# Twelve tiles of a product moved forward into the last two groups of a recurrence

## The reference

```
u = rmsnorm(x) @ w_in                       # 1024 -> 3072
xb, gate = u[..., :1536], u[..., 1536:]
xb = causal_depthwise_conv(xb)              # 4 taps along the sequence
r = sigmoid(xb @ wr + br)                   # 16 blocks of 96 x 96
i = sigmoid(xb @ wi + bi)
a = exp(-8 * r * softplus(-lam))
b = sqrt(1 - a * a) * (i * xb)
hs = scan(h[t] = a[t] * h[t-1] + b[t])      # along the sequence
x = x + (hs * silu(gate)) @ w_out           # 1536 -> 1024, the output product
```

## Time and profile before

| what | value |
|---|---|
| median of three runs | 1154.45 us |
| profiled execution | 1155.51 us |
| its span on the core | 1153.7 us |
| TensorE matmul busy | 1130.5 us, 98% |
| VectorE busy | 637.5 us, 55% |
| ScalarE busy | 519.3 us, 45% |
| GpSimd busy | 159.0 us, 14% |
| granted TensorE clock, mean | 0.996 |
| weight loads | 180 of 512 KB, 3.4 us from issue to landing |

### The profile page before, as it was taken

The page is one execution under the profiler, slowest core; times in us unless marked ns, Lnnn a source line. Parts: engine busy times, 40 slices in busy tenths (PEclk is TensorE's granted clock), DMA queues, the critical chain, the costliest instruction groups (busy, mean ns, idle before and its releaser), DMA issues.

```text
span 1153.7 us, 14370 instructions
## 1 busy us (share of the span) xinstructions
PE 1130.5 (98%) x5342; PEld 889.1 (77%) x5342; DVE 637.5 (55%) x1083; ACT 519.3 (45%) x904; POOL 159.0 (14%) x198
## 2 busy tenths in 40 slices
PE   9999889999999999999999999999999999999997
PEld 6787667887666678867777778888888888888886
DVE  7787887854567665455545544555454232544232
ACT  6656656544566544244434433334443211443231
POOL 2022112310223212032202210012000000000021
PEclk9999999999999999999999999999999999999999
DMA  6323222332111123212223123323223223223312
GB/s 225 110 73 91 92 73 92 110 110 74 55 56 55 37 77 107 97 52 71 91 74 111 59 70 101 101 92 107 95 91 109 92 93 106 90 95 103 98 55 74
DMA packets 30806, 102.82 MB, mean 89 GB/s; under 512 B 3344, under 2 KB 5648, under 8 KB 30736
## 3 DMA queue, kind: packets, MB, share of 16 engines
q1 hardware_dynamic: 30304, 101.37, 27.0%
q10 hardware_dynamic: 432, 0.52, 0.1%
HBM read 99.78 MB, written 2.10 MB: 88 GB/s over the span
## 4 chain that ended last, share of the span: by engine, by line
PE 84%; DVE 9%; ACT 5%; issue 2%; DMA 1%; SPq 0%; DVEq 0%; ACTq 0%
PE ps L693 25%; PE ps L695 24%; PE ps L694 24%; PE ps L817 3%; PE ps L829 2%; PE ps L860 2%; DVE xs L1253 2%; DVE wl L1178 1%; DVE Pt L1384 1%; ACT wh L892 1%; ACT Pt L1057 1%; DVE sg L1269 1%; PE ps L854 1%; DVE cc L1285 1%; PE ps L765 1%
## 5 line engine op out<-in xcount | busy, mean ns | idle before, releaser
L693 PE MATMUL ps<-xgh,wh 128*128 128x512 f32 x848 | 348.8, 411 | 7.9 <-DVE wl L1178 6.9
L695 PE MATMUL ps<-xgh,wl 128*128 128x512 f32 x848 | 332.6, 392 | 0.0
L694 PE MATMUL ps<-xgl,wh 128*128 128x512 f32 x848 | 332.0, 392 | 0.0
L1178 DVE TENSOR_TENSOR wl<-raw,wh 128x1024 fp32r<-128x1024 f32 x180 | 229.5, 1277 | 133.7 <-ACT wh L892 131.9
L892 ACT ACTIVATE wh<-raw 128x1024 fp32r<-128x1024 f32 x180 | 188.5, 1049 | 129.6 <-PE ps L695 128.9
L693 PEld LDWEIGHTS ps<-xgh,wh 128*128 128x128 f32 x848 | 160.1, 189 | 59.0 <-issue 29.5
L695 PEld LDWEIGHTS ps<-xgh,wl 128*128 128x128 f32 x848 | 159.8, 188 | 34.4
L694 PEld LDWEIGHTS ps<-xgl,wh 128*128 128x128 f32 x848 | 160.3, 189 | 32.4 <-issue 3.4
L1638 POOL TENSOR_SCALAR Pt<-Pt,stat 128x256 f32<-128x256 f32 (+2 forms) x128 | 74.7, 596 | 296.4 <-DVE stat L1416 217.8
L1057 ACT ACTIVATE Pt<-Pt,stat 128x256 f32<-128x256 f32 (+2 forms) x128 | 64.7, 506 | 107.6 <-DVE stat L1388 42.2
L693 PE MATMUL ps<-fh,wh 128*128 128x512 f32 x240 | 93.5, 389 | 0.0
(11 more groups left out here) (219 smaller groups left out, 1582.1 us busy)
## 6 DMA issues: line engine op xcount, KB each, us to landing
raw<-wst SPq DMA_DIRECT2D x180, 512.0 KB, 3.4
bst<-nbias SPq DMA_DIRECT2D x8, 256.0 KB, 4.1
xt<-xT SPq DMA_DIRECT2D x3, 512.0 KB, 7.7
outT<-ot SPq DMA_DIRECT2D x2, 384.0 KB, 2.5
outT<-ot SPq DMA_DIRECT2D x6, 128.0 KB, 2.0
raw<-wst SPq DMA_DIRECT2D x2, 256.0 KB, 4.0
cstt<-cst SPq DMA_DIRECT2D x1, 512.0 KB, 5.8
xt<-xT ACTq DMA_DIRECT2D x1, 256.0 KB, 3.6
```

Source lines behind the costliest of these rows:

```text
L693: e.matmul(o, high, a, start=(k == 0), stop=False)
L694: e.matmul(o, high, b, start=False, stop=False)
L695: e.matmul(o, low, a, start=False, stop=stop).then_inc(tile_done, 1)
L1178: e.tensor_tensor(wl_t[:, u % NHL, :], raw_t[:, u % NRAW, :], f32(wh_t[:, u % NHL, :]), ALU.subtract).then_inc(lo_done, 1)
```

## The change

Two accumulators of the output product, `wa` 0 and 1, are opened before the recurrence ends and stay open in banks 7 and 6. In group three their tiles k = 0 to 2 are run, in group four k = 3 to 5: those of `wa` 0 before the conv tiles, those of `wa` 1 between the conv and the gate half. Each of the two groups so holds 64 tiles; the third is tiles 116 to 179, the fourth 180 to 243. Behind the last gates `wa` 0 and 1 run k = 6 to 8 and `wa` 2 and 3 k = 0 to 8 (24 tiles, 244 to 267), and from tile 268 the plan is that of before, in other banks up to 279 and beyond to the end of `wa`. From group three the ring has six banks instead of seven. The due times of the conversions are no longer evenly spaced but tied to the ends of chunks, with one conversion among the taps of each conv chunk; groups three and four hold eight of them, where there were seven. The roots of groups one to three are placed one tick after the next conv chunk's eviction, instead of five ticks after the last gate read.

```diff
+    def take_in(self, name, b):
+        self.bank[name], self.before[name], self.user[b] = b, self.user.get(b), name
...
 def gemm_plan():
     ch = Chunks()
     for g in range(4):
+        if g == 2:
+            ch.ring = 6
+            ch.take_in(("wa", 0), 7)
+        if g > 1:
+            ch.run(("wa", 0), 3 * g - 6, 3 * g - 3, 12)
...
             for c in range(3 * g, 3 * g + 3):
                 ch.one(("conv", c), KD)
+        if g == 2:
+            ch.take_in(("wa", 1), 6)
+        if g > 1:
+            ch.run(("wa", 1), 3 * g - 6, 3 * g - 3, 12)
         for c in range(3 * g, 3 * g + 3):
             ch.one(("silu", c), KD)
         ch.gates(g)
-    ch.seq([("wa", j) for j in range(KD)], 12, 4, 9)
-    ch.ring = 3
+    for j in range(4):
+        if j > 1:
+            ch.take(("wa", j))
+        ch.run(("wa", j), 0 if j > 1 else 6, 9, 12)
+    for j in range(4):
+        ch.run(("wa", j), 9, 12, 12)
+    for j in range(4, KD):
+        ch.one(("wa", j), 12)
+    ch.ring, ch.at = 3, 1
...
-        GROUP = end["conv", 3] + 1 - KD
         UNIT_AT = {1: 4.0, 2: 8.7, 3: 16.0, 4: 23.0}
...
-        for g, j in [(g, j) for g in range(4) for j in range(7)][2:]:
-            UNIT_AT[len(UNIT_AT) + 1] = GROUP * g + 8 * j + (2.2 if g and j in (1, 2) else 7.0)
-            LOW_AFTER[len(UNIT_AT)] = 1.75
+        for g in range(4):
+            places = [end["silu", c] for c in range(3 * g, 3 * g + 3)] + [end["silu", 3 * g + 2] + 8]
+            if g == 0:
+                places = [end["conv", 2]] + places
+            else:
+                taps = [ev_at["conv", c] + 2.0 for c in range(3 * g, 3 * g + 3)]
+                places = [end["conv", 3 * g] - (3 if g > 1 else 0)] + taps + places[g < 2:]
+            for tick in places:
+                UNIT_AT[len(UNIT_AT) + 1] = tick
+                LOW_AFTER[len(UNIT_AT)] = 1.75
...
         def root_tick(g):
-            return gate_tick(3 * g + 2) + 5.0
+            return ev_at["conv", 3 * g + 3] + 1.0 if g < 3 else gate_tick(3 * g + 2) + 5.0
...
                     if k == 0:
                         wait_bank(q, name)
+                        if name == ("wa", 0):
+                            q.wait_ge(rstd_done, 1)
```

More of the change, by code:

```diff
@@ L1697, in weight_stream @@
             full[n, b // 4, j, j] = a[name][0, b]
+    wo = tiles(a["a_w_out"][0])[:, CHUNKS]
     for g in range(4):
+        if g > 1:
+            add(wo[0, 3 * g - 6:3 * g - 3])
         if g == 0:
@@ L1703, in weight_stream @@
             add(conv[3 * g:3 * g + 3])
+        if g > 1:
+            add(wo[1, 3 * g - 6:3 * g - 3])
         add(gate[3 * g:3 * g + 3])
@@ L1717, in weight_stream @@
                 add(over[1:])
-    add_seq(tiles(a["a_w_out"][0])[:, CHUNKS], 4, 9)
+    add(wo[:2, 6:9])
+    add(wo[2:4, :9])
+    add(wo[:4, 9:])
+    add(wo[4:])
     kv, bq = tiles(a["w_kv"]), tiles(a["b_w_in"][0])
```

## The result

The changed kernel takes 1160.51 us (median of six runs, 1160.11 to 1160.59) against 1154.68 us of the kernel before. The ratio is 1.0051, 95% interval 1.0039 to 1.0064: about 5.9 us slower. The profiled executions differ by 4.97 us, 1160.48 against 1155.51, and their spans by 5.0. The profiled execution of the kernel before lies 0.83 us above its median, the changed one's on it, which is the rest of the 5.8 between the medians. The forecast was slower by 4.7 us.

A forecast was written before the change was run, and what follows sets the result against it. The elementwise path through VectorE, ScalarE and GpSimd was taken to bound the groups, not TensorE. Tile 270 at +1.9 us plus 2.8 us of low clock gave +4.7 on a median of 1154.45: 1159.2 us; range +1.5 to +7.5.

The forecast's parts named there:

- The path, not TensorE, paces the groups: Recurrence groups: the elementwise path needs 43.8 us a group, TensorE 41.0; the rival that TensorE paces had chance 0.12.
- Gate reads at 92.1, 138.3 and 184.5: Predicted times of ScalarE's first gate reads of groups two, three and four; the last was 181.78 before.
- An added conversion: An eighth conversion in each of groups three and four is pure delay on VectorE's path: 1.14 us a group.
- The order around the roots: Roots behind ScalarE's conv part, eviction behind a conversion: third tap 1.25 us late in each of two groups; bounds 0 and 1.7.
- The walk: Step-by-step timing of group three with old durations; third tap of chunk 6 at 112.0 instead of 110.74.
- The value of 0.8: Alternative order term a group, if VectorE and GpSimd fully block each other; the result would be 0.9 us lower.
- The tail: Last group's first gate read to end of yl 11: 27.4 us instead of 27.9, bounds 26.7 and 28.4.
- New waits for k = 5 and k = 8: TensorE waits at tiles 182 and 246, about 1 us each; a rival where they delay the path had chance 0.11.
- Tile 270 +1.9: Tile 270, the first needing the last yl, starts at about 212.0 instead of 210.11: 1.9 us later.
- low clock +2.8: Lower clock after TensorE's idle of about 10 us adds 2.8 us, bounds 0 and 3.4; rival without it had chance 0.17.
- Hidden before, all but 1.4: The old kernel's 2.8 us low-clock stretch was off the path, except 1.4 us, which the walk already leaves out.
- The range: The forecast's own range, from +1.5 us (order term 0, clock half) to +7.5 us.

The follow-up runs named there:

- the added work: Kernel before, no tile moved, with 36 matmuls of unused result added in groups three and four: 1153.47 us, ratio 0.9994.
- the order is undone: Two runs of the changed kernel, one with roots due as before, one evicting the chunk before the first conversion in groups three and four: 1156.75 and 1156.53 us.
- the filled wait: Changed kernel with 38 matmuls of unused result added before tiles 268, 269 and 270: 1157.93 us.
- both path edits and the filled wait: Changed kernel with roots early, conversions 34 and 35 behind the last scan, and 26 unused matmuls before tiles 268 to 270: 1152.43 us, ratio 0.9985.
- two conversions late: Changed kernel with conversions 34 and 35 due behind the last scan: 1157.75 us.
- both path edits: Changed kernel with the roots due early and conversions 34 and 35 behind the last scan: 1154.81 us, ratio 1.0005.
- roots early: Changed kernel with the roots of groups one to three due five ticks after the last gate read, as before: 1156.75 us, ratio 1.0023.
- the eviction first: Changed kernel with the first conversion of groups three and four due after the conv chunk's eviction: 1156.53 us, ratio 1.0022.
- one conversion over the gate read: Eviction-first kernel with group three's eighth conversion (unit 24) moved behind group four's first gate products: 1158.79 us.

## Why the prediction was right

It named the right bound, and nearly all its steps have their size.

- *The path, not TensorE, paces the groups.* Right; the added work in the kernel before shows it.
- *Gate reads at 92.1, 138.3 and 184.5.* Measured 92.05, 138.31 and 184.57.
- *An added conversion, 1.14 us a group.* The period is 44.8 where the order is undone and 43.8 before: 1.0. The rows of the third chunk show it where it stands, 4.83 against 3.81.
- *The order around the roots, 1.25 us a group.* 46.26 - 44.8 = 1.45. The size held within the bounds, but the sign by which I wanted to tell it did not: I wrote that the term would be wrong if the third tap of chunk 6 started before 111 us. It started at 110.68. The conversion beside GpSimd's products lost only 0.5 us (1.74 against 1.21), and the tap after it lost the other 1.0 (1.77 against 0.74); the next eviction shows the sum, 112.38 against 111.40 in a group that began 0.47 earlier. The test should have named the eviction. The value of 0.8 that I drew from the Trainium skill ("SBUF — State Buffer", section "SBUF: two separate sides") was too low. I let the conversion shut the third product out, and it ran before the tap was through: GpSimd's three products were over at 111.90 after 4.77 us, and the tap, begun at 110.68, ended at 112.45. The section's blocking whole instructions agrees with these rows; who gets in next was my guess.
- *The tail, 27.4 us.* Measured 27.76: the conversion at 205.79 still held up the last scan, which then met yl (206.68 to 208.13) and took 2.28 us:

```profile
206.93 2.28 DVE L1314 TENSOR_TENSOR_SCAN cc<-aa,xs 128x512 f32<-128x512 f32 x1
```
- *New waits for k = 5 and k = 8, about 1 us each.* 0.26 each. TensorE had not reached them as early as walked.
- *Tile 270 +1.9, low clock +2.8.* Measured +2.36 and +2.62. Both are mis-sized in opposite senses, and that 4.98 lies so near 4.7 owes a little to that. The medians differ by 5.8; the 0.85 above 4.98 is which execution was profiled and no term of the sum. That the clock is a term of its own is shown by the filled wait, -2.6 us. The wait itself was 8.5 us, not 10.
- *Hidden before, all but 1.4.* The old low clock was on the path with the 1.40 us of the gates; with TensorE kept busy the read came 1.79 us earlier, 0.14 of which stood already at the read before, so this was low by about 0.3.
- *The range.* Its low end doesn't follow from the terms: order 0 and half the clock give 4.7 - 2.5 - 1.4 = 0.8, not 1.5. The result lies far from either end.

What was left out: that the two causes of the order term need each other. The walk has both in it and does not say what either costs alone, and the runs show that either alone costs nothing there.

## What to carry to other kernels

Gaps on a busy engine can mean that something else is later, and are then not where time can be won: compare the period of the marks on the other engines (here the first gate read of each group) with the busy engine's own need before filling anything. Work that hides a wait (here the tiles that ran while the last group's path ended) hides less of it when part is moved forward, and what must be prepared for it (here two conversions) goes onto the path earlier as well. When two jobs are shifted in a queue, look for a third that now waits for both in series.

## What the runs showed of the hardware

Two kernels whose profile shows no lower clock in this stretch repeat well: 1153.36 to 1153.77 us over ten runs with the work added, 1152.20 to 1152.72 over eleven with both path edits and the filled wait, against 1152.98 to 1155.77 over 33 of the kernel before. But the changed kernel, with its lower clock, repeats as well, 1160.11 to 1160.59 over six, so a clock that stays up is not the only way to a narrow spread. When the clock comes back after a wait varies: after waits of 8.5, 6.6, 5.4 and 7.7 us before tiles 268 to 270 the next ten tiles took 9.42, 9.22, 8.64 and 8.35 us (changed kernel, two conversions late, both path edits, roots early), which is not the order of the waits. It varies between executions of one kernel too: with the eviction first seven runs with a mean clock of 0.994 or 0.995 took 1156.01 to 1156.73 us, and three at 0.992 took 1157.55 to 1157.92. A gap of 2.23 us was followed by a lower clock in the run with one conversion over the gate read, one of 3.06 us was not in the kernel before.

Beside GpSimd's back-to-back products the cost fell on two VectorE instructions in a row, not only on the one that met them first: of 1.5 us, 0.5 on the conversion and 1.0 on the tap behind it.
